# Narrower expert passes, with the end of one pass woven into the start of the next

## The reference, cut to what matters

```
logits = h @ router                        # 288 tokens x 8 experts
top_v, top_i = top_k(logits, 2)
gate = one_hot(top_i) * softmax(top_v)
for e in range(8):
    out += gate[:, e] * ((silu(h @ w1[e]) * (h @ w3[e])) @ w2[e])
```

## Time and profile before

| | |
|---|---|
| median of 3 runs | 2929.26 us (2928.91 to 2929.31) |
| profiled execution, its own time | 2928.17 us |
| its span, first to last instruction | 2926.4 us |
| mean granted TensorE clock | 0.98 of full |
| TensorE matmuls busy | 2808.3 us, 96% of the span |
| TensorE weight loads busy (beside the matmuls) | 2322.7 us |
| DVE, ACT busy | 855.5 us, 577.7 us |

### The profile page before, as it was taken

The page is one execution under the profiler, slowest core; times in us unless marked ns, Lnnn a source line. Parts: engine busy times, 40 slices in busy tenths (PEclk is TensorE's granted clock), DMA queues, the critical chain, the costliest instruction groups (busy, mean ns, idle before and its releaser), DMA issues. The chain is left out here.

```text
span 2926.4 us, 82143 instructions
## 1 busy us (share of the span) xinstructions
PE 2808.3 (96%) x36778; PEld 2322.7 (79%) x36778; DVE 855.5 (29%) x2362; ACT 577.7 (20%) x1704; POOL 0.2 (0%) x4
## 2 busy tenths in 40 slices
PE   8999989999899999999998999989799999999998
PEld 5777867777777777777786777767699999999997
DVE  2023655555411000102365555541301110110111
ACT  2123323232201000113333323220111111111011
POOL 0000000000000000000000000000000000000000
PEclk9999999999999999999999999989899999999999
DMA  5233432121233434323343111114399899999985
GB/s 214 94 117 146 148 112 74 55 71 61 71 115 123 136 132 134 120 82 136 127 146 121 65 61 65 64 60 135 108 355 365 322 329 366 360 330 348 374 320 222
DMA packets 144474, 496.27 MB, mean 170 GB/s; under 512 B 18608, under 2 KB 23344, under 8 KB 141776
## 3 DMA queue, kind: packets, MB, share of 16 engines
q1 hardware_dynamic: 144208, 492.33, 46.6%
HBM read 471.97 MB, written 20.29 MB: 168 GB/s over the span
## 5 line engine op out<-in xcount | busy, mean ns | idle before, releaser
L365 PEld LDWEIGHTS bank<-work,ring 128*64 128x64 f32 x16896 | 702.1, 137 | 18.5 <-ACT work L2246 11.9
L365 PE MATMUL bank<-work,ring 128*64 128x96 f32 x16896 | 713.0, 247 | 1.2 <-ACT work L2231 0.9
L280 PE MATMUL bank<-hT,ring 128*128 128x288 f32 x2048 | 561.9, 418 | 0.0
L280 PEld LDWEIGHTS bank<-hT,ring 128*128 128x128 f32 x2048 | 376.2, 192 | 100.0 <-ACT work L376 2.7
L358 PE MATMUL bank<-hT,ring 128*128 128x288 f32 x1024 | 256.8, 412 | 7.8 <-PEq L183 7.8
L358 PEld LDWEIGHTS bank<-hT,ring 128*128 128x128 f32 x1024 | 197.3, 193 | 65.3 <-issue 10.1
L1361 ACT ACTIVATE work<-bank 128x256 f32<-128x256 f32 (+3 forms) x272 | 104.5, 396 | 505.5 <-PE bank L1258 119.6
L1732 PE MATMUL bank<-hT,ring 128*128 128x288 f32 x704 | 172.6, 409 | 1.7 <-DVE hT L1806 1.7
L1732 PEld LDWEIGHTS bank<-hT,ring 128*128 128x128 f32 x704 | 134.7, 191 | 39.6 <-issue 2.1
L2289 DVE TENSOR_TENSOR work<-bank,work 128x96 f32<-128x96 f32 x176 | 45.3, 258 | 399.5 <-PE bank L365 399.5
L2242 ACT ACTIVATE work<-bank 128x96 f32<-128x96 f32 x176 | 44.2, 251 | 413.1 <-PE bank L365 413.1
(11 more groups left out here) (401 smaller groups left out, 3068.0 us busy)
## 6 DMA issues: line engine op xcount, KB each, us to landing
ring<-w_ff_dram SPq DMA_DIRECT2D x540, 512.0 KB, 5.3
ring<-w_mix_dram SPq DMA_DIRECT2D x256, 512.0 KB, 3.5
ring<-w_ff_dram SPq DMA_DIRECT2D x72, 384.0 KB, 4.9
work<-s_gla_dram SPq DMA_DIRECT2D x8, 1024.0 KB, 4.8
gla_s_out<-work SPq DMA_DIRECT2D x8, 1024.0 KB, 4.6
work<-s_ret_dram SPq DMA_DIRECT2D x8, 512.0 KB, 4.8
ret_s_out<-work SPq DMA_DIRECT2D x8, 512.0 KB, 3.0
work<-s_rw_dram SPq DMA_DIRECT2D x16, 256.0 KB, 2.7
```

Source lines behind the costliest of these rows:

```text
L280: mm = nc.tensor.matmul(out, ring[:, s, k, :], rhs[:, k, :], start=(k == 0), stop=(k == KT - 1))
L365: mm = nc.tensor.matmul(out[64 * c:64 * c + 64], ring[:, s, k, 64 * c:64 * c + 64], rhs[:, k0 + k, :], start=(k0 + k == 0), stop=(k0 + k = ...
```

## The change

`CAP` becomes 88, so the moving operand of every product of the expert passes, the picking matrices and the ACT and DVE operations on them are 88 wide instead of 96, and the most passes the program allows for becomes 7 instead of 6. The routing phase compares each expert's count with 88 and with every multiple of 88 below 288, which is one comparison and one addition more.

The order of the work around a pass changes in the written-out passes. The transpose of the last output block and the last two matmuls with `scatter` are issued behind the first, second and third slab of the next pass, and the three transposes of `gated` behind its first slab. `scatter` gets a second buffer for that. The seventh and the last pass end with the old order (`finish`). DVE's twelve `choose` operations, which stood ahead of the first product of a pass, are spread over the products 2 to 7, and the three that follow them stand behind product 8. The loop over the w1/w3 slabs runs over slabs 4 to 43, the first four are written out.

```
-CAP = 96
+CAP = 88
...
-                scatter = w(T)
+                scatters = w(2, T)
...
+                def scatter_of(p):
+
+                    return scatters[:, p[1] % 2, :]
...
+                    def to_tokens(p, m):
+
+                        pe.wait_ge(sig("oT"), count(p, KT, m + 3))
+                        pe.wait_ge(sig("otok"), count(p, KT, m + 1))
+                        nc.tensor.transpose(OTOK[0:CAP, 0:128], oT[:, m % 2, :], ident).then_inc(sig("otok_ps"), 1)
+
+                    def add_up(p, m):
+
+                        pe.wait_ge(sig("scatter"), count(p, 1, 1))
+                        pe.wait_ge(sig("otok"), count(p, KT, m + 2))
+                        pe.wait_ge(sig("added"), count(p, KT, m + 1))
+                        mm(ADD[:, 0:T], otok[0:CAP, m % 2, :], scatter_of(p)[0:CAP, :], start=True,
+                           stop=True).then_inc(sig("sc_ps"), 1)
+
+                    def scatter_matrix(p):
 
                         pe.wait_ge(sig("oT"), count(p, KT, 2))
                         pe.wait_ge(sig("picked"), count(p, 1, 1))
                         for i, (a, n) in enumerate(TILES):
                             last = nc.tensor.transpose(SC[0:CAP, a:a + n], gated[0:n, i, :], ident[0:n, 0:n])
                         last.then_inc(sig("scatter_ps"), 1)
+
+                    def finish(p):
+
+                        to_tokens(p, KT - 1)
+                        add_up(p, KT - 2)
+                        add_up(p, KT - 1)
+
+                    def expert(p, before=None):
+
                         pe.wait_ge(sig("hg"), count(p, 1, 1))
                         settle(pe)
+                        up(p, 0, 0)
+                        if before:
+                            to_tokens(before, KT - 1)
+                        scatter_matrix(p)
+                        up(p, 1, 0)
+                        if before:
+                            add_up(before, KT - 2)
+                        up(p, 2, 0)
+                        if before:
+                            add_up(before, KT - 1)
+                        up(p, 3, 0)
                         with pe.Fori(0, UP_SLABS // RING) as g:
-                            for n in range(RING):
+                            for n in range(4, 4 + RING):
                                 up(p, n, g)
...
                     for p in range(FIXED):
-                        expert((0, p))
+                        expert((0, p), (0, p - 1) if p else None)
+                    finish((0, FIXED - 1))
                     with pe.Fori(0, passes(pe)) as i:
                         expert((i, FIXED))
+                        finish((i, FIXED))
...
+                    def take_tokens(p, m):
+
+                        act.wait_ge(sig("otok_ps"), count(p, KT, m + 1))
+                        act.wait_ge(sig("sc_ps"), count(p, KT, m + 1))
+                        ac(otok[0:CAP, m % 2, :], OTOK[0:CAP, 0:128], cp).then_inc(sig("otok"), 1)
+
+                    def expert(p, before=None):
+
+                        if before:
+                            take_tokens(before, KT - 1)
                         act.wait_ge(sig("scatter_ps"), count(p, 1, 1))
-                        act.wait_ge(sig("sc_ps"), count(p, KT, 2))
-                        ac(scatter[0:CAP, :], SC[0:CAP, 0:T], cp).then_inc(sig("scatter"), 1)
+                        act.wait_ge(sig("sc_ps"), count(before or p, KT, 2))
+                        ac(scatter_of(p)[0:CAP, :], SC[0:CAP, 0:T], cp).then_inc(sig("scatter"), 1)
...
+                    def expert(p, before=None):
+
+                        if before:
+                            add_up(before, KT - 2)
+                            add_up(before, KT - 1)
                         dve.wait_ge(sig("picked"), count(p, 1, 1))
-                        choose(count(p, 1, 2))
                         settle(dve)
                         for f in range(FT):
                             dve.wait_ge(slab_done, count(p, FF_SLABS, FF0 + 2 * f + 2))
                             dve.wait_ge(sig("w1_free"), count(p, FT, f + 3))
                             tt(hid[:, f, :], bank[(2 * f + 1) % 4][:, 0:CAP], act1[:, f % 2, :],
                                ALU.mult).then_inc(sig("w3_free"), 1)
-                        for m in range(KT):
-                            dve.wait_ge(sig("sc_ps"), count(p, KT, m + 3))
-                            tt(xT[:, m, :], xT[:, m, :], ADD[:, 0:T], ALU.add).then_inc(sig("added"), 1)
+                            if 2 <= f < 8:
+                                choose(*divmod(f - 2, 3))
+                            if f == 8:
+                                dve.wait_ge(sig("scatter_ps"), count(p, 1, 1))
+                                dve.wait_ge(sig("hg_ps"), count(p, 1, 1))
+                                chosen(count(p, 1, 2))
+                        for m in range(KT - 2):
+                            add_up(p, m)
```

More of the change, by code:

```diff
@@ L2184, in up @@
                         narrow_products(pe, place(p, n), bank[n % 4][:, 0:CAP], hg)
-                    def expert(p):
+                    def to_tokens(p, m):
[9 more added lines that the diff above has]
+                    def scatter_matrix(p):
                         pe.wait_ge(sig("oT"), count(p, KT, 2))
@@ L2195, in expert @@
                         with pe.Fori(0, UP_SLABS // RING) as g:
-                            for n in range(RING):
+                            for n in range(4, 4 + RING):
                                 up(p, n, g)
[L2198 to L2202, removed]
+                        for m in range(KT):
+                            down(p, m)
@@ L2203, in expert @@
                             if m == 2:
                                 gather_tokens(count(p, 1, 2))
[L2205 to L2209, removed]
-                            if m >= 2:
[L2211 to L2215, removed]
+                            if m >= 1:
+                                to_tokens(p, m - 1)
@@ L2217, in _ @@
+                            if m >= 2:
+                                add_up(p, m - 2)
                     grant(pe, sig("sc_ps"), by=2)
@@ L2242, in expert @@
                             ac(act1[:, f % 2, :], bank[2 * f % 4][:, 0:CAP], ACT.Silu).then_inc(sig("w1_free"), 1)
[L2243 to L2246, removed]
+                        for m in range(KT):
+                            act.wait_ge(slab_done, count(p, FF_SLABS, FF0 + UP_SLABS + 3 * m + 3))
+                            ac(oT[:, m % 2, :], DOWN[m % 2][:, 0:CAP], cp).then_inc(sig("oT"), 1)
                             if m >= 1:
-                                act.wait_ge(sig("otok_ps"), count(p, KT, m))
-                                act.wait_ge(sig("sc_ps"), count(p, KT, m))
-                                ac(otok[0:CAP, (m - 1) % 2, :], OTOK[0:CAP, 0:128], cp).then_inc(sig("otok"), 1)
+                                take_tokens(p, m - 1)
                             if m == 3:
@@ L2257, in _ @@
                     for p in range(FIXED):
-                        expert((0, p))
+                        expert((0, p), (0, p - 1) if p else None)
+                    take_tokens((0, FIXED - 1), KT - 1)
                     with act.Fori(0, passes(act)) as i:
                         expert((i, FIXED))
+                        take_tokens((i, FIXED), KT - 1)
                 @block.vector
@@ L2264, in _, with choose, chosen @@
                     tt, ts = nc.vector.tensor_tensor, nc.vector.tensor_scalar
[L2266 to L2274, removed]
+                    def choose(c, i):
+                        ts(pick[:, c, 0, i, :], cst("column"), slot[:, c, i:i + 1], None, ALU.is_equal)
+                        ts(pick[:, c, 1, i, :], cst("column"), slot[:, c, i:i + 1], gate2[:, c, i:i + 1],
+                           ALU.is_equal, ALU.mult).then_inc(sig("pick"), 1)
+                    def chosen(n):
+                        dve.wait_ge(sig("pick"), n * 6)
                         tt(gather, pick[:, 0, 0], pick[:, 1, 0], ALU.add)
@@ L2277, in choose, with add_up @@
                         ts(slot, slot, float(-CAP), None, ALU.add).then_inc(sig("picked"), 1)
-                    def expert(p):
-                        dve.wait_ge(sig("scatter_ps"), count(p, 1, 1))
-                        dve.wait_ge(sig("hg_ps"), count(p, 1, 1))
+                    def add_up(p, m):
+                        dve.wait_ge(sig("sc_ps"), count(p, KT, m + 3))
+                        tt(xT[:, m, :], xT[:, m, :], ADD[:, 0:T], ALU.add).then_inc(sig("added"), 1)
+                    def expert(p, before=None):
+                        if before:
+                            add_up(before, KT - 2)
+                            add_up(before, KT - 1)
                         dve.wait_ge(sig("picked"), count(p, 1, 1))
-                        choose(count(p, 1, 2))
                         settle(dve)
@@ L2290, in expert @@
                                ALU.mult).then_inc(sig("w3_free"), 1)
```

(15 more changed lines are left out.)

## The result

| | before | changed |
|---|---|---|
| median | 2929.28 us (4 runs) | 2887.31 us (2887.16 to 2887.58, 4 runs) |
| span of the profiled run | 2926.4 us | 2885.4 us |

The changed kernel takes 0.9856 of the time of before (95% interval 0.9838 to 0.9873), 42 us less. The prediction was 2870.0 us with a range of 2861 to 2892: inside the range and faster, but 17 us short of the 59 it counted on.

The account below looks back on a forecast made before the run. TensorE was taken to set the pace, with the weights the next bound and close. 65.3 us gone less 6.0 added gave 59.3 off 2928.2, so 2868.9; the median's 1.1 more made 2870.0 us, range 2861 to 2892.

Parts of the forecast that it names:

- Narrower products: Expert products: 3.33 ns less per record, 56.3 us on 16896 records; picking matmuls save 2.9 us more.
- (b): Expert products: narrower columns pay nothing because width counts in steps of 32 or so; 2924 us, chance 0.03.
- (c): Expert loop: a ninth pass runs because an expert has 89 to 96 tokens; 2961 us, chance 0.03.
- The end of a pass: Boundaries into passes 1 to 6: the new order saves 0.82 us each, 4.9 us in all, bounds 0 and 9.
- The cover: Boundaries: slabs of 1.22 us hide ACT's copy and DVE's addition; 1.7 us of cover remain before slab 5.
- The half clock: Stretch at half clock behind one changing boundary: 1.7 us lost there, 1.2 counted as regained, between 0 and 1.7.
- Waits for slabs: TensorE waiting for late expert weights in the w1/w3 slabs: 5 us over eight passes, bounds 0 and 27.
- cushion: Seven slabs between a slot's freeing and next use, 8.5 us, less time to landing: 3.5 us left, 1.3 in the slowest pass.
- What the weights do: Expert weight loads: 430 GB/s asked, at most 408 given, 2.3 us behind per pass; stalls of 5 us in all.
- The upper bound of 27: Weight stalls over eight passes if no cushion helps and 5 us of each pass run at 343 GB/s.
- Rival (a): Expert stage: the weights become the bound, stage 768 us, kernel 2896 us (2889 to 2905); chance 0.13.
- 358 GB/s: Skill's per-core HBM limit: a pass no shorter than 96.7 us, over half the gain lost; the sum went by the trace.

Follow-up runs that it names:

- e3: Changed kernel, but each DMA of expert weights from the stage's ninth slab on loads only half of its slab; 2861.76 us, ratio 0.9768.
- e9: Changed kernel with the w1/w3 loop over slabs 4 to 35, and slabs 36 to 43 written out; 2894.46 us, ratio 0.9879.
- e6: e1 with the w1/w3 loop over slabs 4 to 43 instead of 0 to 39; 2890.72 us, ratio 0.9865.
- e5: Changed kernel, but each expert slab's DMA is issued two slabs later than the slot allows; 2901.99 us, ratio 0.9905.
- e1: Kernel before with 88 slots instead of 96 and nothing else changed, old order kept; 2898.42 us, ratio 0.9895.
- e8: Changed kernel with the next pass's picking matmuls behind block m = 0 of the w2 slabs instead of m = 2; 2877.54 us, ratio 0.9822.

## Why the prediction was right in its direction and short in its size

**Narrower products: right.** Records stand 37.92 ns apart, 3.33 less, with and without the load. 56.3 us, and the picking matmuls' 2.9: a picking step takes 4.50 us without the load of weights, against 4.83 in the quiet passes before. Rivals (b) and (c) are out.

**The end of a pass: right.** The distances at a boundary sum to 3.23 us beyond the regular ones, 3.97 before: 0.74 at six boundaries, 4.4 us for 4.9 predicted. The cover held; no addition or copy is late.

**The half clock: right in part, and low.** In the profiled run of the changed kernel no stretch of the stage is at half clock. Before there were two, and about 1.7 + 1.4 us went with them by the distances; 1.2 was counted. The first lies behind one of the boundaries that change. The second lies behind the seventh, whose order is the old one, and in the repeated run of the changed kernel a stretch at half clock is back there (from 2770.3 us). So its absence, 1.4 us, is luck of that run.

**Waits for slabs: right.** Some 6 us in sum (2.9 in gaps that stand out and about 3 in the steady lag of 0.05 us a slab); 5 were predicted, from the same lag and cushion. The rate was 409 GB/s, and a slab took 8.2 us to landing.

**The step that failed** is that of "What the weights do": it let the queue of weights delay weights only. "I put the stalls at 5 us" is the term, and it measured some 23.5: 6 for slabs, 9.5 inside slabs (10.2 less 0.7 that stood there before beside the half clock) and 8 in the picking step (45.5 us less the 36.0 of e3's, less 1.5 that stood there before). The last two, 17.5 us, are instructions that land too late under the load of the weights. They explain the miss of 17. The upper bound of 27 held by arithmetic for slabs, not by having seen this. The trace before had the hint: its picking step paused in two passes, in waits put down to "issue", under a queue of 5 to 6 us, and both waits end 1.3 to 1.6 us behind a block of instructions. I took them for noise.

In numbers: the stage gave back 56.3 + 2.9 + 4.4 + 3.1 = 66.7 us, and 6 + 17.5 + 0.6 (the first pass's transposes) came, 42.6 by the sum, as measured; each of these terms is good to a few tenths. Outside it 1.6 us came: the matmul of line 1722 ahead of the routing starts 2.7 us later (2069.83 for 2067.15), in code that the change does not touch. In the repeated run of the same kernel it starts at 2067.40, so this differs from run to run.

**Rival (a)** was half right: its stage of 768 us did not come, since the weights' own lateness stayed at 6 us, but through the instructions the weights still took more than a quarter of the forecast gain. One of its arguments was a misreading: the 205 and 109 GB/s behind two boundaries go with DMA shares of 0.64 and 0.31, so the engines had little to do; after the pause of TensorE most slots are loaded, and SP waits for a slab to be used. They say nothing of engines that are slow to come back. The 358 GB/s of the Trainium skill ("DMA: Bandwidth & Descriptors", "Where 436 GB/s comes from") do not bind here: the stage's mean is 361 with the pauses in it, and its stretches run at 409.

**What is shown and what is argued.** Shown: the pauses need the weights' load (e3), end 1.24 to 1.63 us behind the landing of a block of instructions (20 of 21), and follow the placing of the code (e9, and e6 in part). With a shorter queue (e5) they shrink, by less than expected. That a block is late because it stands behind weights in the queue, and not because it is asked for late, is argued from e3 and e5; no view shows when it was asked for. The 11 us between e1 and the changed kernel are not all instructions: in the profiled runs the stages differ by 13.0 us, about 4 of them at the boundaries (28.6 us for 25.0), 4 in e1's stretches at half clock, and the rest late instructions, net of e1's shorter picking steps.

## What to carry to other kernels

When a faster engine raises the demand on a shared queue, ask what else stands in that queue: here 70 small blocks of instructions beside the weights cost three times what the lateness of the weights themselves did. A mean rate below the limit is not enough; put the work that asks for nothing where the reserve is lowest (e8: one digit changed, 10 us), and keep straight code out of the stretch in which the queue is longest, by letting a loop run up to its end (e9: a loop that ends eight slabs earlier cost 5 to 7 us). Where a wait names nothing in a DMA-heavy stage, count the instruction blocks before calling it noise.

## What the hardware showed that I had not expected

TensorE pauses for 0.2 to 1.3 us in the middle of slabs whose weights had landed 0.8 to 6 us before, and goes on 1.24 to 1.63 us after a block of instructions has landed. The changed kernel and e3 differ in bytes alone, and their picking steps take 5.9 and 4.5 us. A loop over 32 slabs instead of 40, with 84 instead of 70 blocks fetched, costs 5 to 7 us at full load.
